# A decoder step with a width-31 depthwise convolution: one channel tile moves from GpSimd to products with diagonals on TensorE

## The chip, the cores and the metric

The kernel runs on one core of one Trainium2 chip. The metric is the device time of one execution in microseconds, the median of several runs. A core has five engines with queues of their own: TensorE (PE), VectorE (DVE), ScalarE (ACT), GpSimd (POOL) and SyncE (SP). [...] In this kernel SP does nothing but issue DMAs, in the order of its program.

## The reference

One inference step of two layers over 512 prompt tokens and 8 x 8 sample tokens, 576 columns in all, with 1024 channels, float32. Layer 0 mixes tokens with a recurrent state (RWKV), layer 1 with a causal Conformer convolution module; after each comes a gated feed-forward part with its own width-3 convolution. The change is in layer 1's mixer:

```
def _causal_dwconv(x, buf, w, b):            # w: (31, 1024), one filter of 31 taps for each channel
    xp = concatenate([buf, x], axis=1)       # 30 earlier rows in front (zeros for the prompt)
    y = depthwise_conv(xp, w)                # y[t, c] = sum over n of w[n, c] * xp[t + n, c]
    return y + b, xp[:, -30:]                # the last 30 rows are an output, the new state

def _conformer_conv(x, buf, w_in, b_in, dw_w, dw_b, ln_w, ln_b, w_out, b_out):
    h = x @ w_in + b_in                      # 1024 -> 2048
    h = h[..., :C] * sigmoid(h[..., C:])     # gated linear unit (glu)
    h, new_buf = _causal_dwconv(h, buf, dw_w, dw_b)
    h = silu(layernorm(h, ln_w, ln_b))       # mean and variance over the 1024 channels
    return h @ w_out + b_out, new_buf
```

## The kernel before, in words

Everything is held with channels on the 128 partitions, so 1024 channels are eight channel tiles (`KT`) of 128 x 576. The order of the work on each engine is written out by hand in one program per engine; a counting semaphore stands for each kind of event. The semaphore `tile_full` counts the PSUM tiles that PE has filled, `tile_read` those that another engine has read out; PSUM holds four tiles, and `begin(t)` in PE's program waits until tile t - 4 is read. `TB[name]` is the running number of the first tile of a step.

The mixer of layer 1 runs like this:

- `glu`: PE makes 16 products (L471 and L472, 512 and 64 columns), two for each channel tile. ACT evicts them to `gsig`, the second with a sigmoid (L1122, L1124). DVE multiplies the two and puts the result into `gb` (L1570, L1572), behind 30 columns of history; `glu_ready` counts the channel tiles.
- The depthwise convolution is divided by channel tile. DVE makes tiles 0, 2, 4, 6, 7 with 31 taps each, and the last 11 taps of tile 5: a tap is one multiply-add on 512 columns and one on 64 (L1615; the first tap of a tile L1617). DVE keeps two tiles in turn and does one glu step at every 16th tap. POOL makes tile 1: it multiplies into a scratch tile `ptmp` and adds that (L1706, L1707, L1711). PE makes the first 20 taps of tile 5 and all of tile 3, each tap a product of a 128 x 128 diagonal of the tap's weights with the shifted columns, summed up in PSUM (L797, L798). The diagonals come from ACT (L1117), a few ahead of each glu pair; ACT evicts the two PSUM tiles, adding the bias (L1127).
- `go`: DVE copies the newest rows of every channel tile together (`newest`, L1581 and L1583), PE transposes them (L483), ACT reads the two tiles into `ost` (L1131, L1133). SP then stores them: 73 DMAs, which are 8 for the prompt, 64 for the samples, and one copy of the older rows from input to output. Behind them SP loads the weights of `co` into a ring of four buffers.
- `ln`: PE sums the eight channel tiles with a matrix of 1/1024 (in the order 0, 2, 4, 6, 3, 1, 7, 5, each term waiting for its tile), ACT copies the mean (L1135), DVE subtracts it (L1630), ACT squares (L855), PE sums again, DVE takes the reciprocal (L1175) and scales (L1634), ACT applies silu (L1140).
- `co`: PE multiplies with the output weights, waiting for its first weight tile and for silu; then norms, the second feed-forward part, and the outputs.

What sets the order of SP's part:

```
            eng.wait_ge(sm["tile_read"], TB["go"] + 2)
            for kt in range(KT):
                store(out["p_glu"]...)
                for b in range(DB):
                    store(out["s_glu"]...)
            store(out["s_glu"][0, :, 0:NSTATE - DS, :], a["state_conv_glu"][0, :, DS:NSTATE, :])
            weights("co", a["conv_w_out"][0], range(KT))
```

Of the kernel before, what the change touches and what calls it, by code (L numbers as in the profile page):

```python
# [24 lines left out]
ALU = mybir.AluOpType  # L25
# [4 lines left out]
P = 128  # L30
D = 1024
SEQ = 512
DB, DS = 8, 8
DEC = DB * DS
T = SEQ + DEC
KT = D // P
# [4 lines left out]
CW = 31  # L41
# [83 lines left out]

DW_DVE, DW_POOL, DW_PE = (0, 2, 4, 6, 7), 1, (5, 3)
DW_TAPS = {5: 20, 3: CW}
DW_JOBS = [(kt, n) for kt in DW_PE for n in range(DW_TAPS[kt])]  # L130


# [6 lines left out]
TB = {}  # L139
# [31 lines left out]
A_FR = A_FO  # L171
# [5 lines left out]
A_SIG = A_CO + REG  # L177
GLU_EVERY = 16
A_DIAG = A_SIG + 2 * T
A_PTMP = A_DIAG + len(DW_JOBS) * P  # L180
assert A_PTMP + T <= A_FR
NSOUT = 2 * DB


def build(nc, a, out):
    with ExitStack() as ctx:
# [6 lines left out]
        def sem(name):  # L193
            return ctx.enter_context(nc.semaphore(name))
# [19 lines left out]
        def region(at, n=KT, w=T):  # L214
            return arena[:, at:at + n * w].rearrange("p (k t) -> p k t", t=w)
# [17 lines left out]
        gb = region(A_GB, KT, GB)  # L233
        gst = arena[:, A_GR:A_GR + NGS]
        cvo = region(A_CO)
        gsig = region(A_SIG, 2)
        gd = gb[:, :, NSTATE + SEQ:GB].rearrange("p k (b t) -> p k b t", b=DB)
# [29 lines left out]
        def pcol(name, i):  # L267
            return par[:, PCOL[name] + i:PCOL[name] + i + 1]

        def gain(n, kt):  # L270
# [3 lines left out]
                 "tile_full", "tile_read", "sq_ready", "sq_used", "x_ready", "h_ready", "xm_ready", "vec_done",  # L274
                 "v_ready", "wide_ready", "prep_sq", "prep_s", "prep_done", "kn_ready", "unit_done", "gath_ready",
                 "rk_ready", "sel_ready", "rstd_ready", "z_ready", "zeroed", "sd_turned", "sd_ready", "rf_ready",
                 "rows_ready", "snat_ready", "state_out", "glu_ready", "conv_done", "conv_pool", "pool_tap",
                 "diag_ready", "ln_v"]
        sm = {n: sem(n) for n in NAMES}
        w_in = [sem(f"w_in{i}") for i in range(RING)]  # L280
# [12 lines left out]
        def tset(t):  # L293
            return (t % 4) * 1024
# [163 lines left out]
        def _(pe):  # L458
# [5 lines left out]
            def product(t, terms, m=P, mark=None):  # L464

                begin(t)
                for i, (lhs, rhs, pre) in enumerate(terms):
                    for w, v in pre:
                        pe.wait_ge(w, v)
                    st, sp = i == 0, i == len(terms) - 1  # L470
                    pe.matmul(ps[0:m, tset(t):tset(t) + SEQ], lhs, rhs[:, 0:SEQ], start=st, stop=sp)  # L471
                    ins = pe.matmul(ps[0:m, tset(t) + SEQ:tset(t) + T], lhs, rhs[:, SEQ:T], start=st, stop=sp)  # L472
                    if mark is not None and not sp:
                        ins.then_inc(mark, 1)
                ins.then_inc(sm["tile_full"], 1)
# [177 lines left out]
            for k in range(KT):  # L653
                g, b = k % 2, 0
# [54 lines left out]
            for kt in range(KT):  # L709
                t = TB["pz"] + 3 * kt  # L710
# [79 lines left out]
            for m, kt in enumerate(DW_PE):  # L790
                t = TB["dw"] + m
                begin(t)
                pe.wait_ge(sm["glu_ready"], kt + 1)
                for n in range(DW_TAPS[kt]):
                    pe.wait_ge(sm["diag_ready"], job + 1)
                    st, sp = n == 0, n == DW_TAPS[kt] - 1
                    pe.matmul(ps[:, tset(t):tset(t) + SEQ], diag[:, job, :], gb[:, kt, n:n + SEQ], start=st, stop=sp)  # L797
# [10 lines left out]
            by = {kt: (sm["conv_done"], m + 1) for m, kt in enumerate(DW_DVE + DW_PE[:1])}  # L808

            by[DW_DVE[-1]] = by[DW_PE[0]]  # L810
            by[DW_PE[1]] = (sm["tile_read"], TB["dw"] + 2)
            by[DW_POOL] = (sm["conv_pool"], 1)
            product(TB["ln"], [(con[:, C_MEAN:C_MEAN + P], cvo[:, kt, :], [by[kt]]) for kt in (0, 2, 4, 6, 3, 1, 7, 5)])
            norm_sums("ln", first=1)
            gemm("co", cvo, (sm["z_ready"], KT))
# [344 lines left out]
        def _(dve):  # L1160
# [8 lines left out]
            def after():  # L1169
                if done[0]:  # L1170
                    dve.wait_ge(sm["vec_done"], done[0])
# [302 lines left out]
            for kt in range(KT):  # L1474
                t = TB["pz"] + 3 * kt
                g, b = tmp[:, 2 * (kt % 2), :], tmp[:, 2 * (kt % 2) + 1, :]
# [112 lines left out]

            turned, done_glu, step, waiting, active, last = False, 0, 0, [(kt, 0) for kt in DW_DVE] + [(DW_PE[0], DW_TAPS[DW_PE[0]])], [], {}  # L1590
            while waiting or active:
# [3 lines left out]
                while len(active) < 2 and waiting and waiting[0][0] < done_glu:  # L1595
                    kt, n = waiting.pop(0)
# [11 lines left out]
                kt, n = active.pop(0)  # L1608
                cd = cvo[:, kt, SEQ:T].rearrange("p (b t) -> p b t", b=DB)
                w = pcol("conv_dw_w", n * KT + kt)  # L1610
# [13 lines left out]
                    active.append([kt, n + 1])  # L1624
            dve.wait_ge(sm["tile_read"], TB["ln"] + 1)
            dve.wait_ge(sm["conv_done"], len(DW_DVE) + 1)
            dve.wait_ge(sm["conv_pool"], 1)
            after()
            for kt in range(KT):
                v.tensor_tensor(cvo[:, kt, :], cvo[:, kt, :], tmp[:, 3, :], ALU.subtract).then_inc(sm["ln_v"], 1)  # L1630
# [9 lines left out]
        @block.gpsimd  # L1640
        def _(pool):
            p = nc.gpsimd
            def ffn(l):
                w = FF[l]
                st = fst[:].rearrange("p (b w f) -> p b w f", b=DB, w=2)

                def decode(j):
                    return raw[:, j, 2 + SEQ:RAW].rearrange("p (b t) -> p b t", b=DB)

                def w_lo(at, i=None):  # L1650

                    pool.wait_ge(w["w_hi"], at + 1 + (0 if i is None else i * 4))
                    p.tensor_tensor(wsplit[:, at % 4, 1], ring[:, at % 2], wsplit[:, at % 4, 0].bitcast(F32), ALU.subtract)\  # L1653
                        .then_inc(w["w_lo"], 1)

                def tails(i, j):

                    pool.wait_ge(sm["tile_read"], i * 4 + (t0 + at + j + 1))
                    f = (j % 2) * FT + j // 2 + f0
                    o = fo[:, bass.ds(i * 2 + f, 1), :]  # L1660
                    p.tensor_copy(o[:, :, 0:2], raw[:, j:j + 1, SEQ:SEQ + 2]).then_inc(w["tails"], 1)
                    p.tensor_copy(o[:, :, 2:18].rearrange("p o (b t) -> p (o b) t", t=2), decode(j)[:, :, DS:DS + 2])\
                        .then_inc(w["tails"], 1)

                t0 = TB[f"f{l}"]
                for n in range(LOOK):
                    w_lo(n)
                pool.wait_ge(w["no_hist"], 4)
                pool.wait_ge(sm["tile_read"], TB[f"fst{l}"] + 2)
                for j in range(4):  # L1670
                    p.tensor_copy(decode(j)[:, :, 0:2], st[:, :, :, (j % 2) * FT + j // 2]).then_inc(w["hist_ready"], 1)
                at = 0
                for part, (f0, nf) in enumerate(PARTS):
                    last = part == len(PARTS) - 1
                    with pool.Fori(0, nf // 2 - last) as i:
                        for j in range(4):
                            w_lo(at + j + LOOK, i)
                            tails(i, j)

                            pool.wait_ge(w["conv_ready"], i * 4 + (2 * f0 + j + 1))  # L1680
                            pool.wait_ge(w["tails"], i * 8 + (4 * f0 + 2 * j + 2))
                            f = (j % 2) * FT + j // 2 + 2 + f0
                            src = st[:, :, :, bass.ds(i * 2 + f, 1)].rearrange("p b w o -> p b (w o)")
                            p.tensor_copy(decode(j)[:, :, 0:2], src).then_inc(w["hist_ready"], 1)  # L1684
                    if last:
                        for j in range(4):
                            w_lo(at + 2 * nf - 4 + j + LOOK)
                            tails(nf // 2 - 1, j)
                    at += 2 * nf
                    for n in range(KT):  # L1690
                        if at + n + LOOK < NFFN:
                            w_lo(at + n + LOOK)
                    at += KT

            ffn(0)

            kt = DW_POOL
            ptmp = arena[:, A_PTMP:A_PTMP + T]
            pool.wait_ge(sm["glu_ready"], kt + 1)
            for n in range(CW):  # L1700
                dst = ptmp if n else cvo[:, kt, :]
                w = pcol("conv_dw_w", n * KT + kt)
                add = pcol("conv_dw_b", kt) if n == 0 else 0.0
                if n > 1:
                    pool.wait_ge(sm["pool_tap"], 2 * n - 1)
                p.tensor_scalar(dst[:, 0:SEQ], gb[:, kt, n:n + SEQ], w, add, ALU.mult, ALU.add)  # L1706
                p.tensor_scalar(dst[:, SEQ:T].rearrange("p (b t) -> p b t", b=DB), gd[:, kt, :, n:n + DS], w, add, ALU.mult, ALU.add)\  # L1707
                    .then_inc(sm["pool_tap"], 1)
                if n:
                    pool.wait_ge(sm["pool_tap"], 2 * n)  # L1710
                    p.tensor_tensor(cvo[:, kt, :], cvo[:, kt, :], ptmp, ALU.add)\  # L1711
                        .then_inc(sm["pool_tap"] if n < CW - 1 else sm["conv_pool"], 1)
            ffn(1)


# [29 lines left out]
```

## Time and profile before

| what | us |
|---|---|
| median of three runs (2418.45 to 2422.42) | 2419.24 |
| span of the profiled execution, first to last instruction | 2418.1 |
| PE busy in it | 2176.1 (90%) |
| DVE busy | 1328.9 (55%) |
| ACT busy | 564.9 (23%) |
| POOL busy | 512.5 (21%) |

The profile is of one execution. Its times count from the span's start, and a busy engine is not always the one that the others wait for: the share on the chain of work that ended last says more. The mixer of layer 1 lies between 1555 and 1875 us. In the rows below an engine's "idle before" stands in square brackets, with the instruction that ended it; a queue with a q at the end (SPq) is the part of an engine that issues. One fp32 product has two rows in the trace (x2). [...]

### The profile page before, as it was taken

Reading aid. Unit: us, or ns where it says so; the run is one execution under the profiler, and the core shown is the slowest. Engines: PE = TensorE matmul, PEld = TensorE weight load, DVE = VectorE, ACT = ScalarE, POOL = GpSimd, SP = SyncE. Lnnn points to the kernel's source line nnn. Section 1 sums busy time; section 2 is a strip of 40 time slices with the busy share of each in tenths; the row PEclk is TensorE's granted clock in tenths of the full one; section 3 lists DMA queues with packets and bytes.
Section 4 is the critical chain, followed back from the end, with each engine's and each line's share of the span. In section 5 each row is a group of like instructions: output and inputs, shape, how many; then the busy total and the mean of one; then the engine's idle time right before and its main releaser. Section 6 shows DMA issues by size and latency. Waiting matters only on the chain.

```text
span 2418.1 us, 33008 instructions
## 1 busy us (share of the span) xinstructions
PE 2176.1 (90%) x12995; PEld 1753.6 (73%) x12995; DVE 1328.9 (55%) x2206; ACT 564.9 (23%) x903; POOL 512.5 (21%) x496
## 2 busy tenths in 40 slices
PE   5999999999998699979799998799959797999985
PEld 3555579999997345569799898555535597998985
DVE  5127345556665833078548365469970586284563
ACT  3203133232222020133222222321020432122122
POOL 0000000000000000024445343059200144354440
PEclk8999899999999876989899999899979898999998
DMA  4022100000000030112222221221011022222221
GB/s 128 21 60 60 35 1 10 10 1 10 1 10 1 0 85 9 50 44 70 86 72 78 88 70 53 66 61 42 1 54 53 26 79 78 75 82 79 79 61 46
DMA packets 228490, 116.90 MB, mean 48 GB/s; under 512 B 26065, under 2 KB 226217, under 8 KB 228233
## 3 DMA queue, kind: packets, MB, share of 16 engines
q1 hardware_dynamic: 228377, 115.31, 16.8%
q8 instruction: 81, 1.33, 0.2%
q14 instruction: 32, 0.26, 0.0%
HBM read 109.33 MB, written 6.67 MB: 48 GB/s over the span
## 4 chain that ended last, share of the span: by engine, by line
PE 62%; DVE 21%; issue 12%; ACT 3%; DVEq 1%; DMA 1%; POOL 0%; ACTq 0%; SPq 0%; POOLq 0%
PE ps L471 23%; PE ps L727 19%; PE ps L553 14%; DVE arena L1615 6%; PE ps L472 4%; DVE arena L1532 1%; DVE arena L1528 1%; DVE arena L1537 1%; DVE arena L1511 1%; DVE arena L1365 1%; ACT hidsplit L1083 1%; DVE tmp L1419 1%; DVE tmp L1175 1%; DVE arena L1512 1%; DVE tmp L1436 1%
## 5 line engine op out<-in xcount | busy, mean ns | idle before, releaser
L1653 POOL TENSOR_TENSOR wsplit<-arena,wsplit 128x1024 fp32r<-128x1024 f32 x136 | 325.4, 2393 | 1456.0 <-ACT wsplit L1053 1456.0
L727 PE MATMUL ps<-hsplit,wsplit 128*128 128x288 f32 x4224 | 575.9, 298 | 21.3 <-POOL wsplit L1653 19.8
L471 PE MATMUL ps<-arena 128*128 128x512 f32 (+4 forms) x1024 | 572.1, 642 | 18.2 <-ACT arena L1140 6.4
L727 PEld LDWEIGHTS ps<-hsplit,wsplit 128*128 128x128 f32 x4224 | 569.4, 190 | 24.3 <-POOL wsplit L1653 22.4
L553 PE MATMUL ps<-arena 128*128 128x128 f32 (+2 forms) x2992 | 392.8, 285 | 46.7 <-DVE arena L1365 14.9
L553 PEld LDWEIGHTS ps<-arena 128*128 128x128 f32 x2992 | 359.3, 194 | 76.9 <-DVE arena L1365 19.9
L472 PEld LDWEIGHTS ps<-arena 128*128 128x128 f32 (+4 forms) x1024 | 198.0, 193 | 261.4 <-issue 261.4
L727 PE MATMUL ps<-hidsplit,wsplit 128*128 128x288 f32 x2112 | 296.0, 304 | 48.9 <-DVE hidsplit L1541 48.9
L727 PEld LDWEIGHTS ps<-hidsplit,wsplit 128*128 128x128 f32 x2112 | 294.0, 196 | 50.3 <-DVE hidsplit L1541 50.3
L1053 ACT ACTIVATE wsplit<-arena 128x1024 fp32r<-128x1024 f32 x136 | 139.1, 1052 | 223.2 <-PE ps L727 212.5
L1615 DVE SCALAR_TENSOR_TENSOR arena<-arena,par 128x512 f32<-128x512 f32 x322 | 175.1, 623 | 0.1
L471 PEld LDWEIGHTS ps<-arena 128*128 128x128 f32 (+4 forms) x1024 | 158.3, 195 | 19.3 <-issue 18.7
L472 PE MATMUL ps<-arena 128*128 128x64 f32 (+4 forms) x1024 | 172.3, 251 | 0.0
L1175 DVE RECIPROCAL tmp<-tmp 128x576 f32<-128x576 f32 x9 | 33.8, 3753 | 228.6 <-ACT tmp L863 228.6
L1531 DVE SCALAR_TENSOR_TENSOR arena<-arena,par 128x512 f32<-128x512 f32 x176 | 140.1, 796 | 26.2 <-DVE arena L1528 6.7
L1527 DVE TENSOR_SCALAR arena<-arena,par 128x512 f32<-128x512 f32 x88 | 140.0, 1591 | 18.5 <-DVE arena L1513 18.5
L926 ACT ACTIVATE arena<-arena 64x256 f32<-64x256 f32 x148 | 61.4, 415 | 213.3 <-PE ps L553 211.0
L1551 DVE TENSOR_TENSOR arena<-arena,ps 128x576 f32<-128x576 f32 x32 | 24.1, 754 | 147.8 <-PE ps L727 147.8
L1083 ACT ACTIVATE hidsplit<-arena 128x576 f32 x44 | 30.2, 687 | 255.4 <-DVE arena L1537 255.4
L553 PE MATMUL ps<-tmp,arena 128*128 128x128 f32 (+2 forms) x432 | 86.6, 314 | 0.4 <-ACT arena L982 0.4
L1237 DVE SCALAR_TENSOR_TENSOR arena<-arena,par 128x576 f32<-128x576 f32 x48 | 35.4, 811 | 92.5 <-PE ps L472 92.4
L1684 POOL COPY arena<-arena 128x16 f32 x80 | 38.9, 486 | 200.6 <-DVE arena L1532 200.6
(203 smaller groups left out, 2012.5 us busy)
## 6 DMA issues: line engine op xcount, KB each, us to landing
arena<-ffn_w_in SPq DMA_DIRECT2D x88, 512.0 KB, 3.9
arena<-ffn_w_out SPq DMA_DIRECT2D x32, 512.0 KB, 4.0
arena<-conv_w_in SPq DMA_DIRECT2D x16, 512.0 KB, 4.0
arena<-ffn_w_out SPq DMA_DIRECT2D x16, 384.0 KB, 3.3
arena<-rwkv_wk SPq DMA_DIRECT2D x8, 512.0 KB, 5.7
arena<-rwkv_wr SPq DMA_DIRECT2D x8, 512.0 KB, 4.0
arena<-rwkv_wv SPq DMA_DIRECT2D x8, 512.0 KB, 3.9
arena<-rwkv_wo SPq DMA_DIRECT2D x8, 512.0 KB, 5.0
```

The source lines that it names most:

```text
L471: pe.matmul(ps[0:m, tset(t):tset(t) + SEQ], lhs, rhs[:, 0:SEQ], start=st, stop=sp)
L472: ins = pe.matmul(ps[0:m, tset(t) + SEQ:tset(t) + T], lhs, rhs[:, SEQ:T], start=st, stop=sp)
L553: return pe.matmul(o, lhs, rhs, start=start, stop=stop)
L727: ins = pe.matmul(ps[:, s + 512 * z:s + 512 * z + HALF], lhs(u, i), rhs[:, v, i, HALF * z:HALF * z + HALF], start=i == 0 and n == 0, stop= ...
L926: ins = f(dst[e:e + 64, k, e:e + 64], src[e:e + 64, k, tok], ACT.Copy)
L1053: f(wsplit[:, at % 4, 0], ring[:, at % 2], ACT.Copy).then_inc(FF[l]["w_hi"], 1)
L1083: f(hidsplit[:, 0, bass.ds(i * 2 + q, 1), :], cv[:, 2 * q:2 * q + 1, :], ACT.Copy).then_inc(w["hid_hi"], 1)
L1175: seq(v.reciprocal(tmp[:, 2, :], tmp[:, 2, :]))
L1527: v.tensor_scalar(cv[:, j, 0:SEQ], rp[:, 0:SEQ], tap(0), bias, ALU.mult, ALU.add).then_inc(chain, 1)
L1531: v.scalar_tensor_tensor(cv[:, j, 0:SEQ], rp[:, n:n + SEQ], tap(n), cv[:, j, 0:SEQ], ALU.mult, ALU.add).then_inc(chain, 1)
L1615: ins = v.scalar_tensor_tensor(dst, src, w, dst, ALU.mult, ALU.add)
L1653: p.tensor_tensor(wsplit[:, at % 4, 1], ring[:, at % 2], wsplit[:, at % 4, 0].bitcast(F32), ALU.subtract)\
```

## The change

Channel tile 1 is taken from POOL and given to PE as a third tile of the list `DW_PE`, with all 31 taps. POOL's loop, its scratch tile and its two semaphores go. What follows from the list follows without further edits: the number of diagonals rises from 51 to 82 (`DW_JOBS`), so ACT makes 11 instead of 7 ahead of each glu pair (five ahead of the last); PE has three depthwise tiles in PSUM (`TILES`, `("dw", len(DW_PE))`), ACT evicts three; the waits of the LayerNorm sum and of DVE for tile 1 are now on that eviction. DVE's program is the same but for this one wait.

```diff
--- before.py
+++ after.py
@@ -125,8 +125,8 @@
 
 
 
-DW_DVE, DW_POOL, DW_PE = (0, 2, 4, 6, 7), 1, (5, 3)
-DW_TAPS = {5: 20, 3: CW}
+DW_DVE, DW_PE = (0, 2, 4, 6, 7), (5, 3, 1)
+DW_TAPS = {5: 20, 3: CW, 1: CW}
 DW_JOBS = [(kt, n) for kt in DW_PE for n in range(DW_TAPS[kt])]
 
 
@@ -177,8 +177,7 @@
 A_SIG = A_CO + REG
 GLU_EVERY = 16
 A_DIAG = A_SIG + 2 * T
-A_PTMP = A_DIAG + len(DW_JOBS) * P
-assert A_PTMP + T <= A_FR
+assert A_DIAG + len(DW_JOBS) * P <= A_FR
 NSOUT = 2 * DB
 
 
@@ -274,7 +273,7 @@
                  "tile_full", "tile_read", "sq_ready", "sq_used", "x_ready", "h_ready", "xm_ready", "vec_done",
                  "v_ready", "wide_ready", "prep_sq", "prep_s", "prep_done", "kn_ready", "unit_done", "gath_ready",
                  "rk_ready", "sel_ready", "rstd_ready", "z_ready", "zeroed", "sd_turned", "sd_ready", "rf_ready",
-                 "rows_ready", "snat_ready", "state_out", "glu_ready", "conv_done", "conv_pool", "pool_tap",
+                 "rows_ready", "snat_ready", "state_out", "glu_ready", "conv_done",
                  "diag_ready", "ln_v"]
         sm = {n: sem(n) for n in NAMES}
         w_in = [sem(f"w_in{i}") for i in range(RING)]
@@ -809,7 +808,7 @@
 
             by[DW_DVE[-1]] = by[DW_PE[0]]
             by[DW_PE[1]] = (sm["tile_read"], TB["dw"] + 2)
-            by[DW_POOL] = (sm["conv_pool"], 1)
+            by[DW_PE[2]] = (sm["tile_read"], TB["dw"] + 3)
             product(TB["ln"], [(con[:, C_MEAN:C_MEAN + P], cvo[:, kt, :], [by[kt]]) for kt in (0, 2, 4, 6, 3, 1, 7, 5)])
             norm_sums("ln", first=1)
             gemm("co", cvo, (sm["z_ready"], KT))
@@ -1624,7 +1623,7 @@
                     active.append([kt, n + 1])
             dve.wait_ge(sm["tile_read"], TB["ln"] + 1)
             dve.wait_ge(sm["conv_done"], len(DW_DVE) + 1)
-            dve.wait_ge(sm["conv_pool"], 1)
+            dve.wait_ge(sm["tile_read"], TB["dw"] + 3)
             after()
             for kt in range(KT):
                 v.tensor_tensor(cvo[:, kt, :], cvo[:, kt, :], tmp[:, 3, :], ALU.subtract).then_inc(sm["ln_v"], 1)
@@ -1694,22 +1693,6 @@
 
             ffn(0)
 
-            kt = DW_POOL
-            ptmp = arena[:, A_PTMP:A_PTMP + T]
-            pool.wait_ge(sm["glu_ready"], kt + 1)
-            for n in range(CW):
-                dst = ptmp if n else cvo[:, kt, :]
-                w = pcol("conv_dw_w", n * KT + kt)
-                add = pcol("conv_dw_b", kt) if n == 0 else 0.0
-                if n > 1:
-                    pool.wait_ge(sm["pool_tap"], 2 * n - 1)
-                p.tensor_scalar(dst[:, 0:SEQ], gb[:, kt, n:n + SEQ], w, add, ALU.mult, ALU.add)
-                p.tensor_scalar(dst[:, SEQ:T].rearrange("p (b t) -> p b t", b=DB), gd[:, kt, :, n:n + DS], w, add, ALU.mult, ALU.add)\
-                    .then_inc(sm["pool_tap"], 1)
-                if n:
-                    pool.wait_ge(sm["pool_tap"], 2 * n)
-                    p.tensor_tensor(cvo[:, kt, :], cvo[:, kt, :], ptmp, ALU.add)\
-                        .then_inc(sm["pool_tap"] if n < CW - 1 else sm["conv_pool"], 1)
             ffn(1)
```

On PE, this is the place between the last tap of tile 3 and the LayerNorm sum. Lines L797 and L798 are the taps (L796 and L797 after the change, where the file is one line shorter above), L483 (L482) the transposes of `go`, L471 (L470) the first term of the sum. Before:

```order
L797 MATMUL ps<-arena 128x512 [waits diag_ready]
L798 MATMUL ps<-arena 128x64
L483 MATMUL ps<-con,arena 120x128 [waits tile_read,gath_ready]
L483 MATMUL ps<-con,arena 120x128
L483 MATMUL ps<-con,arena 128x128 [waits tile_read]
L483 MATMUL ps<-con,arena 128x128 x3
L471 MATMUL ps<-arena,con 128x512 [waits conv_done,tile_read]
```

And after it, from the last tap of tile 3 into the first taps of tile 1:

```order
L796 MATMUL ps<-arena 128x512 [waits diag_ready]
L797 MATMUL ps<-arena 128x64
L796 MATMUL ps<-arena 128x512 [waits diag_ready,glu_ready,tile_read]
L797 MATMUL ps<-arena 128x64
L796 MATMUL ps<-arena 128x512 [waits diag_ready]
L797 MATMUL ps<-arena 128x64
```

Where the transposes stood, 31 pairs for tile 1 begin; the transposes and the sum follow behind them.

On ACT, the rows from the last but one glu pair to the copy of the mean (L1117 diagonals, L1122 and L1124 glu evictions, L1127 depthwise evictions, L1131 and L1133 the reads of `go`, L1135 the mean). Before:

```order
L1117 ACTIVATE arena<-con,par 128x128 x7
L1122 ACTIVATE arena<-ps,par 128x576 [waits tile_full,glu_ready]
L1124 ACTIVATE arena<-ps,par 128x576 [waits tile_full]
L1117 ACTIVATE arena<-con,par 128x128 x2
L1122 ACTIVATE arena<-ps,par 128x576 [waits tile_full,glu_ready]
L1124 ACTIVATE arena<-ps,par 128x576 [waits tile_full]
L1127 ACTIVATE arena<-ps,par 128x576 [waits tile_full] x2
L1131 ACTIVATE ost<-ps 120x256 [waits out_done,tile_full]
L1133 ACTIVATE ost<-ps 128x512 [waits tile_full]
L1135 ACTIVATE tmp<-ps 128x576 [waits tile_full]
```

And after it, the same stretch, one line number lower:

```order
L1116 ACTIVATE arena<-con,par 128x128 x11
L1121 ACTIVATE arena<-ps,par 128x576 [waits tile_full,glu_ready]
L1123 ACTIVATE arena<-ps,par 128x576 [waits tile_full]
L1116 ACTIVATE arena<-con,par 128x128 x5
L1121 ACTIVATE arena<-ps,par 128x576 [waits tile_full,glu_ready]
L1123 ACTIVATE arena<-ps,par 128x576 [waits tile_full]
L1126 ACTIVATE arena<-ps,par 128x576 [waits tile_full] x3
L1130 ACTIVATE ost<-ps 120x256 [waits out_done,tile_full]
L1132 ACTIVATE ost<-ps 128x512 [waits tile_full]
L1134 ACTIVATE tmp<-ps 128x576 [waits tile_full]
```

More diagonals stand ahead of each pair, and a third eviction stands between PE's depthwise tiles and the reads of `go`. SP's program is word for word the same.

## Rows read from the trace of the kernel before

**Rows 1.** The page: the span, and the chain that ended last by engine

```profile
span 2418.1 us, 33008 instructions
...
PE 62%; DVE 21%; issue 12%; ACT 3%; DVEq 1%; DMA 1%; POOL 0%; ACTq 0%; SPq 0%; POOLq 0%
```

**Rows 2.** Windows of PE: stretch, length, busy, granted clock, DMA share, GB/s

```profile
1564.37:1751.70 187.33, 187.31 (x694) 1.00 0.13 36
1751.70:1760.40 8.70, 0.00 (x0) 0.67 0.00 0
1769.90:1781.04 11.14, 0.01 (x1) 0.73 0.07 16
1781.04:1785.55 4.51, 4.49 (x8) 0.52 0.06 14
1785.55:1798.40 12.85, 10.52 (x32) 0.87 0.62 181
```

**Rows 3.** Waits of PE, 1550 to 1810: total, times, longest

```profile
PE ps L471 <- DVE arena L1615: 11.1, 1, 11.1
PE ps L483 <- DVE arena L1583: 8.8, 1, 8.8
```

**Rows 4.** Timeline of PE: start, us, line, shapes, count [idle before]

```profile
1696.34 1.08 PE L797 MATMUL ps<-arena 128*128 128x512 f32 x2
...
1751.35 0.33 PE L798 MATMUL ps<-arena 128*128 128x64 f32 x2
1760.44 1.53 PE L483 MATMUL ps<-con,arena 128*120 128x128 f32 x6 [8.77 <-DVE arena L1583]
...
1804.80 2.05 PE L471 MATMUL ps<-arena 128*128 128x512 f32 x2 [6.41 <-ACT arena L1140]
```

**Rows 5.** Windows of the tap line L1615 alone, before and while POOL works

```profile
1577.16:1593.40 16.24, 12.96 (x30) 1.00 0.21 60
1628.99:1652.30 23.31, 23.31 (x32) 1.00 0.22 64
```

**Rows 6.** Timeline of DVE: two glu steps and the last taps

```profile
1576.16 0.69 DVE L1570 TENSOR_TENSOR arena<-arena 128x512 f32<-128x512 f32 x1 [13.09 <-ACT arena L1124]
...
1593.47 0.69 DVE L1570 TENSOR_TENSOR arena<-arena 128x512 f32<-128x512 f32 x1 [2.67 <-ACT arena L1124]
...
1760.30 20.69 DVE L1615 SCALAR_TENSOR_TENSOR arena<-arena,par 128x512 f32<-128x512 f32 x48
```

**Rows 7.** Windows of POOL: its tile

```profile
1594.00:1710.00 116.00, 109.78 (x92) 1.00 0.15 45
```

**Rows 8.** Timeline of ACT: diagonals, a glu eviction, a depthwise eviction, the reads of go

```profile
1576.03 2.15 ACT L1117 ACTIVATE arena<-con,par 128x128 f32<-128x128 f32 x7
1584.10 0.74 ACT L1122 ACTIVATE arena<-ps,par 128x576 f32<-128x576 f32 x1 [5.92 <-PE ps L472]
...
1751.71 0.74 ACT L1127 ACTIVATE arena<-ps,par 128x576 f32<-128x576 f32 x1 [32.79 <-PE ps L798]
1761.16 0.39 ACT L1131 ACTIVATE ost<-ps 120x256 f32<-120x256 f32 x1 [8.71 <-PE ps L483]
1762.01 0.60 ACT L1133 ACTIVATE ost<-ps 128x512 f32<-128x512 f32 x1 [0.47 <-PE ps L483]
```

**Rows 9.** Timeline of SP: the first stores, a slower eight, the weights of co

```profile
1762.64 0.33 SPq L348 DMA_DIRECT2D out_p_glu<-ost  x1
1763.01 2.66 SPq L348 DMA_DIRECT2D out_s_glu<-ost  x8
...
1766.08 2.94 SPq L348 DMA_DIRECT2D out_s_glu<-ost  x8
...
1788.74 53.45 SPq L303 DMA_DIRECT2D arena<-conv_w_out  x8
```

**Rows 10.** Landing of conv_w_out tiles: the first one alone, then all eight

```profile
DMA to landing us min/median/max: 7.5/7.5/7.5
...
DMA to landing us min/median/max: 3.7/5.6/9.9
```

## The prediction

> **What bounds the stage now.** I read the page first, then TensorE's (PE's) busy time by stretch, its waits and its timeline, then VectorE (DVE), GpSimd (POOL), ScalarE (ACT) and SyncE (SP) in the same 250 us, because the diff touches only the depthwise stage and what comes right behind it. The page says that PE carries 62% and DVE 21% of the chain that ended last [rows 1]. So PE leads nearly everywhere, and this stage is a place where DVE takes over.
>
> The stretches show where. PE is busy without a gap at granted clock 1.00 from 1564.37 to 1751.70: the glu product, and from 1696.34 the two depthwise tiles. Then it does nothing for 8.70 us, works 9.5 us, and does nothing for 11.14 us [rows 2]. The two idle stretches are the waits for DVE of 8.8 and 11.1 us [rows 3]: the first for the gathered newest rows (L1583), the second for DVE's last tap (L1615). DVE's last block of taps starts at 1760.30 and lasts 20.69 us, to 1781.0 [rows 6]; PE resumes at 1781.04 with the last two terms of the LayerNorm sum. The reader is to see that DVE ends last here, with some 20 us of PE time free in front of it, and that POOL is not the one waited for: its tile is done by 1710 [rows 7].
>
> A second chain runs beside it, on SP. Its first store of the glu state goes out at 1762.64, 0.03 us after ACT's second read of the `go` tiles ended (1762.01 + 0.60). Seventy-three stores (8 + 64 + 1) follow one another, and only behind them, at 1788.74, the first weight tile of the next product `co` [rows 8, 9]. That tile takes 7.5 us to land [rows 10], so it is there at 1796.2. PE starts `co` at 1804.80 [rows 4] because the normalized input comes then. The weights have 8.6 us of slack.
>
> **The change part by part.**
>
> *PE gains a third product.* The two existing ones are 51 taps from 1696.34 to 1751.35 + 0.33 = 1751.68 [rows 4], 55.34 us or 1.085 us a tap, across POOL's end. Thirty-one more are 33.64 us. They stand in front of the `go` transposes, so PE ends its taps at 1751.68 + 33.64 = 1785.32 where it ended at 1751.68. Nothing in front of them gets earlier: PE was already without a gap from 1564.37 on, so a faster DVE gives the glu product nothing. The free 8.70 + 11.14 = 19.8 us cover part; the rest sticks out.
>
> *ACT gains 31 diagonals and one eviction.* Seven diagonals take 2.15 us and ACT then idles 5.92 us until its next tile [rows 8]; eleven take 3.4 us. Cost nothing, hidden by that idle time; without the cover it would be 1.2 us for each of seven glu pairs. The eviction (0.74 us, as the one at 1751.71 [rows 8]) lies between the product's end and the reads of `go`.
>
> *POOL loses its tile, DVE gets faster.* POOL worked 109.8 us of the 116 us in which it made the tile [rows 7]. A DVE tap, one instruction on 512 and one on 64 columns, costs 12.96 / 15 = 0.864 us before POOL starts, 23.31 / 16 = 1.46 us while it works, and 20.69 / 24 = 0.862 us afterwards [rows 5, 6]. So DVE gets back some half a microsecond on each tap that ran beside POOL. It cannot use all of it, since a glu step stands behind every 16 taps and these come from PE 17.31 us apart (1576.16, 1593.47 [rows 6]), and 16 × 0.864 us and a glu step of under a microsecond, less than 15 us, is less. The eighth glu step then falls at 1576.16 + 7 × 17.31 = 1697.3, with 96 of the 5 × 31 + 11 = 166 taps done; the other 70 take 60.4 us, and the glu step and the copies of the newest rows about a microsecond each: DVE ends near 1759.8, 21 us earlier. The newest rows, with 24 taps behind them, are ready near 1738. Both now wait for PE, so this gain is worth nothing on the path.
>
> [...]
>
> *Chain one, through the LayerNorm.* From 1785.32 PE does six transposes (0.8 us, half of the 1.53 us that they took right after an idle stretch [rows 4]) and all eight terms of the sum, now without waiting: the third tile's eviction is done 0.8 us after the product, behind transposes and five other terms. A term has the shapes of a tap, so eight are 8 × 1.085 = 8.7 us, and the sum is there at 1794.8 instead of 1785.5: 9.3 us later. [...] So 1.8 us come back, and the input of `co` is ready 7.5 us later, at 1812.3.
>
> *Chain two, through SP.* SP issues in order and its wait is on the `go` tiles, which now lie behind the third product. Product ends 1785.32, ACT evicts it (0.74), reads the first `go` tile (0.39) and the second (0.60): 1787.1. The first store goes out there instead of at 1762.64, 24.4 us later. The stores are the same, 26.10 us of issue, so the first weight tile is issued at 1813.2 and lands 7.5 us on, at 1820.7. That is behind the 1812.3 of chain one: the weights' slack of 8.6 us is used up and they become what PE waits for. `co` starts at 1820.7 instead of 1804.80, **15.9 us later**. The next tiles are issued right behind it and none landed later than 9.9 us after its issue [rows 10]; PE takes 8 × 1.085 us for each product, so they do not add. PE begins `co` after an idle stretch in either case. Behind `co` nothing that the diff touches is left and every step follows its predecessor as before, so the delay stays to the end.
>
> Bounds: eight stores took 2.66 to 2.94 us, so the stores are 0.3 us less to 2.3 us more; a `conv_w_out` tile landed in 3.7 to 9.9 us [rows 10], so −3.8 to +2.4 us. I take the first tile's own landing, 7.5 us, because the same copy of older rows stands in front of it. Ends: 11.8 to 20.6 us.
>
> **Sum.** The profiled span is 2418.1 us; the runs' median, 2419.24, is 1.1 us above it. 2418.1 + 15.9 = 2434.0 of span, 2435.1 as a median. Own range 2430 to 2440.
>
> **Rivals.**
>
> B: only chain one counts, because the weights come in time (SP's stores go out faster, or the first tile lands early enough). Then +7.5, 2426.7 us. For it: the LayerNorm chain is what decides now. Against it: it wants 8.4 us less in the stores and the landing, and the even rows of the stores leave 0.3 and the fastest landing 3.8.
>
> C, the other side: the third product disappears in PE's idle stretches and DVE's 21 us count. Place: PE between 1751.7 and 1781.0. With taps that cost nothing the sum ends right behind DVE, and `co` starts with the weights at 1751.7 + 1.8 + 26.1 + 7.5 = 1787.1, so 2401 us; at half the price they come at 1803.9, 2418 us. It decides at 0.57 us a tap, where the weights come at 1804.8 as `co` does now. Against it: 102 rows of this very line at 1.085 us a tap with PE at full clock.
>
> D: the granted clock falls under a longer unbroken stretch. It stood at 1.00 for 187 us, and the stretch becomes some 230. At the low clock in the added taps, +34 us more, 2469 us. No row of this stage speaks for it.
>
> **Chances.** Forecast 0.86, B 0.07, C 0.03, D 0.04. A measurement of this kernel can tell about 0.2%, 4.8 us, from no change. A, B and D are slower by more, 0.95 with a little of B below the line; C is 0.03 faster and the remaining 0.02 same. The range reaches from B to the upper bound of the forecast: 2426 to 2440.
>
> **What would show it.** In the profile of the changed kernel: taps in a row of 82 at 1.085 us ending near 1785; no wait of PE for L1615 or the newest rows; DVE taps at 0.86 us throughout, ending near 1760, with waits of 2 to 3 us at each glu step; the first glu store near 1787, the first `conv_w_out` issue near 1813; PE idle for about 15 us before `co`, with ACT's normalized input done some 8 us before that idle ends. I am wrong if `co` starts when ACT's input comes (B), if PE does not reach the transposes near 1785 (C or D), or if a later stage takes the 16 us back.

## The result and the profile after

| kernel | median us | runs | ratio to the kernel before, 95% interval |
|---|---|---|---|
| before | 2420.83 | 4 | |
| changed | 2436.32 (2435.27 to 2438.1) | 4 | 1.0069, 1.0055 to 1.0083 |

The changed kernel is slower by 15.5 us by the medians. The prediction was 2435.1 us, 15.9 us over the median of three runs that it started from. The profiled executions differ a little more, 2435.0 against 2418.1 us of span: 16.9 us.

The page of the changed kernel, its chain that ended last by engine (the row of before is in [rows 1]):

```profile
PE 67%; DVE 15%; issue 12%; ACT 3%; DVEq 1%; SPq 1%; DMA 1%; POOL 0%; ACTq 0%; POOLq 0%
```

PE's share rises from 62% to 67%, DVE's falls from 21% to 15%: the stage in which DVE took over has gone to PE. SPq, at 0% before, now has 1%: the issue queue of SP has come onto the chain.

PE's waits in the mixer, 1550 to 1830 (total, times, longest), to be read beside [rows 3]:

```profile
PE ps L470 <- DMA arena<-conv_w_out: 15.5, 1, 15.5
PE ps L470 <- DVE arena L1183: 5.6, 1, 5.6
PE ps L470 <- ACT tmp L854: 2.3, 1, 2.3
```

Both waits for DVE in this stage, 8.8 and 11.1 us, are gone; the 5.6 us are those ahead of the glu product, which were there before. In their place is a wait that did not exist: 15.5 us for the DMA of the `co` weights.

PE's stretches, as in [rows 2] (length, busy, granted clock as a share of full speed, DMA share, GB/s):

```profile
1564.37:1785.50 221.13, 221.13 (x823) 1.00 0.11 31
1785.50:1794.60 9.10, 9.09 (x37) 1.00 0.05 13
1796.90:1805.80 8.90, 8.84 (x32) 1.00 0.07 18
1805.80:1821.29 15.49, 0.00 (x1) 0.62 0.40 118
```

The reader is to see one unbroken stretch of 221 us at clock 1.00, up to the end of the third product, then the LayerNorm sums at 1.00 too, and then 15.5 us with nothing.

PE's timeline at both ends of that (columns as in [rows 4]):

```profile
1785.00 0.33 PE L797 MATMUL ps<-arena 128*128 128x64 f32 x2
1785.17 0.82 PE L482 MATMUL ps<-con,arena 128*120 128x128 f32 x6
...
1821.29 2.05 PE L470 MATMUL ps<-arena 128*128 128x512 f32 x2 [15.52 <-DMA arena<-conv_w_out]
...
1823.44 2.02 PE L470 MATMUL ps<-arena 128*128 128x512 f32 x2
...
1825.58 1.53 PE L470 MATMUL ps<-arena 128*128 128x512 f32 x2
...
1827.11 1.08 PE L470 MATMUL ps<-arena 128*128 128x512 f32 x2
```

The last tap ends at 1785.33, the six transposes take 0.82 us, and `co` starts at 1821.29 where it started at 1804.80: 16.5 us later.

DVE's first instruction of the stage (the scaling of the norm ahead of the glu products), in the kernel before and then in the changed one:

```profile
1554.74 5.92 DVE L1184 SCALAR_TENSOR_TENSOR arena<-x,par,tmp 128x576 f32<-128x576 f32 x8
```

```profile
1554.82 5.92 DVE L1183 SCALAR_TENSOR_TENSOR arena<-x,par,tmp 128x576 f32<-128x576 f32 x8
```

From there to the first `co` product it is 250.1 us before and 266.5 us after, 16.4 us more. This length, called the stage's length below, is given for the experiments too, because their profiled executions differ by up to 3.1 us in what lies ahead of the stage.

DVE's timeline, two glu steps, taps behind them, and the last taps (columns as in [rows 6]):

```profile
1593.59 0.69 DVE L1569 TENSOR_TENSOR arena<-arena 128x512 f32<-128x512 f32 x1 [2.67 <-ACT arena L1123]
...
1594.45 12.96 DVE L1614 SCALAR_TENSOR_TENSOR arena<-arena,par 128x512 f32<-128x512 f32 x30
...
1628.20 0.69 DVE L1569 TENSOR_TENSOR arena<-arena 128x512 f32<-128x512 f32 x1 [15.54 <-ACT arena L1123]
...
1738.63 20.68 DVE L1614 SCALAR_TENSOR_TENSOR arena<-arena,par 128x512 f32<-128x512 f32 x48
```

Thirty instructions, 15 taps, take 12.96 us where POOL used to work beside them (19.62 us before for the same 30), and DVE ends at 1738.63 + 20.68 = 1759.3 instead of 1781.0. It now waits 2.6 to 3.5 us at a usual glu step and 15.54 us at the fourth, in front of which it has only one tap to do.

ACT's timeline: diagonals, the third depthwise eviction, the two reads of `go`, the first silu (columns as in [rows 8]):

```profile
1576.15 3.31 ACT L1116 ACTIVATE arena<-con,par 128x128 f32<-128x128 f32 x11
1584.22 0.74 ACT L1121 ACTIVATE arena<-ps,par 128x576 f32<-128x576 f32 x1 [4.76 <-PE ps L471]
...
1785.37 0.74 ACT L1126 ACTIVATE arena<-ps,par 128x576 f32<-128x576 f32 x1 [32.80 <-PE ps L797]
1786.01 0.38 ACT L1130 ACTIVATE ost<-ps 120x256 f32<-120x256 f32 x1
1786.27 0.60 ACT L1132 ACTIVATE ost<-ps 128x512 f32<-128x512 f32 x1
...
1811.16 6.18 ACT L1139 ACTIVATE arena<-arena,par 128x576 f32<-128x576 f32 x8 [3.10 <-DVE arena L1633]
```

Eleven diagonals take 3.31 us and still leave 4.76 us of idle time (5.92 us before). The first silu starts at 1811.16; before, `co` followed it by 1.02 us.

SP's timeline, the first stores, the slowest eight, the weights (columns as in [rows 9]), and under it the landing of the first two weight tiles (us from issue, minimum, median, maximum):

```profile
1786.90 0.33 SPq L347 DMA_DIRECT2D out_p_glu<-ost  x1
1787.27 2.66 SPq L347 DMA_DIRECT2D out_s_glu<-ost  x8
...
1806.37 3.23 SPq L347 DMA_DIRECT2D out_s_glu<-ost  x8
...
1813.58 45.46 SPq L302 DMA_DIRECT2D arena<-conv_w_out  x8
```

```profile
DMA to landing us min/median/max: 7.6/8.2/8.9
```

The stores begin at 1786.90 instead of 1762.64 and take 26.7 us of issue; 1813.58 and 7.6 us are 1821.2, when PE starts.

### The profile page after: what moved, and what is told of

The parts are those of the page before. It is cut to its first block, busy times and chain, and to the rows that moved or that the text cites. A ratio compares the mean times of both kernels' runs of the same rounds, so it can differ in the third digit from the quotient of the medians.

```text
span 2435.0 us, 33195 instructions
## 1 busy us (share of the span) xinstructions
PE 2203.4 (90%) x13119; PEld 1769.5 (73%) x13119; DVE 1288.1 (53%) x2206; ACT 573.7 (24%) x935; POOL 402.5 (17%) x404
## 3 DMA queue, kind: packets, MB, share of 16 engines
q8 instruction: 82, 1.34, 0.2%
## 4 chain that ended last, share of the span: by engine, by line
PE 67%; DVE 15%; issue 12%; ACT 3%; DVEq 1%; SPq 1%; DMA 1%; POOL 0%; ACTq 0%; POOLq 0%
PE ps L470 25%; PE ps L726 19%; PE ps L552 14%; PE ps L471 4%; PE ps L796 3%; DVE arena L1531 1%; DVE arena L1527 1%; DVE arena L1536 1%; DVE arena L1510 1%; DVE arena L1364 1%; SPq L347 1%; ACT hidsplit L1082 1%; DVE tmp L1418 1%; DVE arena L1511 1%; DVE tmp L1435 1%
## 5 line engine op out<-in xcount | busy, mean ns | idle before, releaser
L470 PE MATMUL ps<-arena 128*128 128x512 f32 (+4 forms) x1024 | 572.9, 643 | 27.3 <-DMA arena<-conv_w_out 15.5
L726 PE MATMUL ps<-hsplit,wsplit 128*128 128x288 f32 x4224 | 576.0, 298 | 21.3 <-POOL wsplit L1652 19.8
L471 PEld LDWEIGHTS ps<-arena 128*128 128x128 f32 (+4 forms) x1024 | 198.1, 193 | 261.8 <-issue 261.8
L470 PEld LDWEIGHTS ps<-arena 128*128 128x128 f32 (+4 forms) x1024 | 158.7, 196 | 28.5 <-issue 27.8
L471 PE MATMUL ps<-arena 128*128 128x64 f32 (+4 forms) x1024 | 172.5, 251 | 0.0
L1530 DVE SCALAR_TENSOR_TENSOR arena<-arena,par 128x512 f32<-128x512 f32 x176 | 140.1, 796 | 26.2 <-DVE arena L1527 6.7
L1614 DVE SCALAR_TENSOR_TENSOR arena<-arena,par 128x512 f32<-128x512 f32 x322 | 139.1, 507 | 0.1
L796 PE MATMUL ps<-arena 128*128 128x512 f32 x164 | 88.1, 619 | 0.0
```

The costliest lines, as they stand in the source:

```text
L726: ins = pe.matmul(ps[:, s + 512 * z:s + 512 * z + HALF], lhs(u, i), rhs[:, v, i, HALF * z:HALF * z + HALF], start=i == 0 and n == 0, stop= ...
L1530: v.scalar_tensor_tensor(cv[:, j, 0:SEQ], rp[:, n:n + SEQ], tap(n), cv[:, j, 0:SEQ], ALU.mult, ALU.add).then_inc(chain, 1)
L1614: ins = v.scalar_tensor_tensor(dst, src, w, dst, ALU.mult, ALU.add)
```

## The experiments

Each experiment was measured in turn with the kernel before on the same chip, whose median there was 2420 to 2421 us; ratios are to it. The theory is that of the prediction: PE's third product puts off the `go` tiles, SP's order puts the weights of `co` behind them and 73 stores, and DVE's regained time is off the path.

**The weights ahead of the stores.** On SP, in the changed kernel:

```diff
+            weights("co", a["conv_w_out"][0], range(KT), upto=RING)
             eng.wait_ge(sm["tile_read"], TB["go"] + 2)
             ...
-            weights("co", a["conv_w_out"][0], range(KT))
+            weights("co", a["conv_w_out"][0], range(KT), first=RING)
```

> Changed kernel, but SP issues the first four weight tiles of co ahead of its wait for the go tiles, so ahead of the 73 stores. Theory (the weights behind the stores set the start of co): co starts when ACT's normalized input is there, which in the changed kernel was 9.1 us before PE got its weights (ACT's silu from 1811.2, co from 1821.3), so 2436.3 - 9 = 2427 us. Rival (the third product alone is the delay, and the weights only happen to come at that time): within 1 us of the changed kernel, 2436 us.

Measured: 2427.78 us, 1.0029 (1.0018 to 1.004). Its waits of PE from 1690 to 1835, and SP's first weights and first store:

```profile
PE ps L471 <- ACT arena L1140: 6.4, 1, 6.4
PE ps L471 <- ACT tmp L855: 2.3, 1, 2.3
```

```profile
1689.75 4.82 SPq L302 DMA_DIRECT2D arena<-conv_w_out  x4
1784.09 0.36 SPq L347 DMA_DIRECT2D out_p_glu<-ost  x1
```

The 15.5 us wait for the DMA is gone and PE waits for ACT's silu again, 6.4 us as before the change. By the medians, 8.5 of the 15.5 us by which the kernel had become slower were SP's order; the remaining 7 are the LayerNorm chain behind the third product, the 7.5 us of the prediction's chain one. The stage's length, 257.4 us (1552.01 to 1809.36), says the same: 9.1 us less than in the changed kernel, 7.3 us more than before.

**The same edit in the kernel before.**

> Kernel before with the same reordering on SP alone. Theory: its weights had 8.6 us of slack, so nothing moves, 2420 to 2422 us. Rival (the order on SP is worth the same in any version, for instance because the stores disturb the weight loads): about 9 us faster, 2412 us.

Measured: 2420.09 us, 1.0001 (0.9992 to 1.001). The stage's length is 250.1 us, as without the edit. The order on SP costs nothing there; its weights had slack, and the change used it up.

**POOL kept busy.** The changed kernel, with POOL doing its old loop on tile 1 into a buffer that nobody reads:

```diff
+            pool.wait_ge(sm["glu_ready"], kt + 1)
+            for n in range(CW):
+                dst = ptmp if n else idle            # idle, ptmp: hg[:, 0, :], hg[:, 1, :]
+                p.tensor_scalar(dst[:, 0:SEQ], gb[:, kt, n:n + SEQ], w, add, ALU.mult, ALU.add)
+                ...
```

> Changed kernel, but POOL does its old loop of tile 1 into a buffer that nobody reads. Theory (PE and then SP set the end, so DVE's 21 us are off the path): DVE's taps take 1.3 to 1.5 us again beside POOL and end near 1781, and the time stays within 1.5 us of the changed kernel, 2436 us. Rival (DVE's gain already pays for part of the third product): up to 21 us slower, 2446 to 2457 us.

Measured: 2434.69 us, 1.0068 (1.0054 to 1.0082), which is not to be told from the changed kernel. DVE's last taps and its next instruction, and PE's wait:

```profile
1758.02 20.67 DVE L1614 SCALAR_TENSOR_TENSOR arena<-arena,par 128x512 f32<-128x512 f32 x48
1793.07 5.44 DVE L1629 TENSOR_TENSOR arena<-arena,tmp 128x576 f32<-128x576 f32 x8 [14.37 <-ACT tmp L1134]
```

```profile
PE ps L470 <- DMA arena<-conv_w_out: 15.3, 1, 15.3
```

DVE's taps ended at 1778.7 there, in an execution in which the stage lay 2.2 us earlier, so some 21.6 us later than in the changed kernel, and no engine waited for it: PE reached the sum's last terms only behind its third product, and its wait is still the one for the weights. The stage's length is 266.2 us for 266.5. What DVE gained from an idle POOL was worth nothing in the changed kernel.

**One tap instead of 31.** `DW_TAPS[1] = 1`: the third product and its PSUM tile stay, with one tap and its diagonal; the other 30 diagonals go with their taps.

> Changed kernel with one tap instead of 31 in tile 1's product; the other 30 taps are left out of the output. Theory (33.6 us of PE, 1.085 us a tap, are the whole price; the order on SP then decides): PE ends its taps near 1753, DVE near 1760, the first store goes out near 1754.6, the weights land near 1788.3 and co starts there, 16.4 us before the kernel before: 2404 us. Rival (something else of the change costs the time, the diagonals or the third PSUM tile): not below 2415 us. Second rival (the stores do not matter): co starts near 1780, 2396 us.

Measured: 2401.96 us, 0.9926 (0.9911 to 0.9941). PE's transposes of `go` and the start of `co`, and SP's weights:

```profile
1749.62 0.83 PE L482 MATMUL ps<-con,arena 128*120 128x128 f32 x6
...
1785.68 2.04 PE L470 MATMUL ps<-arena 128*128 128x512 f32 x2 [13.78 <-DMA arena<-conv_w_out]
```

```profile
1778.06 7.45 SPq L302 DMA_DIRECT2D arena<-conv_w_out  x4
```

Thirty taps less are 34.4 us less by the medians, against 30 × 1.085 = 32.6 us of products. The stage's length, 1551.73 to 1785.68, is 234.0 us, 32.5 us less than in the changed kernel, so the products account for all of it there. The price lies in the taps, not in the list of three or its PSUM tile. This run does not separate a tap from its diagonal; that the diagonals cost nothing is read from the changed kernel's trace, where PE runs through all 82 taps without a wait, busy for 88.99 of the 88.99 us from 1696.34 to 1785.33. And `co` still starts with the weights, 7.6 us after their issue, though ACT's silu began at 1777.29: this kernel too waits for SP's order. What it would gain without that, an estimate of 7.4 us from the 1.02 us between silu and `co` elsewhere, was not measured.

**Tile 1 divided between PE and DVE.** PE makes 15 taps of tile 1, DVE the other 16 behind PE's eviction, POOL stays idle; the LayerNorm sum takes the tiles that DVE ends last at its end. Once with the weights ahead of the stores, once without.

```diff
-DW_DVE, DW_PE = (0, 2, 4, 6, 7), (5, 3, 1)
-DW_TAPS = {5: 20, 3: CW, 1: CW}
+DW_DVE, DW_PE = (0, 2, 4, 6, 7), (5, 1, 3)
+DW_TAPS = {5: 20, 1: 15, 3: CW}
...
-[(kt, 0) for kt in DW_DVE] + [(DW_PE[0], DW_TAPS[DW_PE[0]])]
+[(kt, 0) for kt in DW_DVE] + [(kt, DW_TAPS[kt]) for kt in DW_PE[:2]]
```

> POOL idle as in the changed kernel, but tile 1 is divided: PE makes its first 15 taps (order on PE: tile 5 with 20 taps, tile 1 with 15, tile 3 with 31) and DVE the other 16, and the first four weight tiles of co are issued ahead of the stores. Theory (DVE's regained 21 us are worth something once PE does not carry the whole tile, and the weights are out of the way): PE ends its taps at 1751.7 + 15 x 1.085 = 1768, DVE near 1774.4, the LayerNorm sum ends near 1777.5 instead of 1785.5 and the second sum saves 1.8 us more, so co starts 9 to 10 us before the kernel before: 2411 us. Rival (DVE's regained time is lost in its waits for glu steps and for PE's partial tile): not faster than before, 2418 to 2422 us.

> The same division of tile 1, with SP's order as it was. Theory (the weights follow the go tiles by 1.8 + 26.1 + 7.5 us): the go tiles come at 1768 instead of 1751.7 plus DVE's wait, the weights near 1803.5, so co starts about 1 us before the kernel before: 2419 us. Rival (the stores do not matter here): 2411 us, as with the weights first.

Measured: 2411.93 us, 0.9965 (0.9952 to 0.9979) with the weights first; 2420.22 us, 1.0001 (0.9992 to 1.001) without. The start of `co` in the first and in the second:

```profile
1794.54 2.05 PE L471 MATMUL ps<-arena 128*128 128x512 f32 x2 [6.41 <-ACT arena L1139]
```

```profile
1802.95 2.05 PE L470 MATMUL ps<-arena 128*128 128x512 f32 x2 [15.04 <-DMA arena<-conv_w_out]
```

With the weights out of the way the division pays, 8.6 us by the medians against the kernel before: DVE, faster without POOL (12.96 us for 15 taps, 0.864 us each), can take 16 of tile 1's taps off PE. With the old order on SP the same division gains nothing: PE waits 15.0 us for the DMA. Both came within 1.3 us of what was expected.

**DVE without waits for glu pairs.** The balanced version with the weights first, in an order in which DVE always has a tile at hand:

```diff
-DW_DVE, DW_PE = (0, 2, 4, 6, 7), (5, 1, 3)
-DW_TAPS = {5: 20, 1: 15, 3: CW}
-GLU_EVERY = 16
+DW_DVE, DW_PE = (0, 1, 2, 4, 6), (5, 7, 3)
+DW_TAPS = {5: 2, 7: 18, 3: CW}
+GLU_EVERY = 19
```

> As the balanced version with the weights first, but DVE's order is changed so that it always has a tile to work on while it waits for glu pairs: DVE makes tiles 0, 1, 2, 4, 6 with a glu step at every 19th tap (19 x 0.864 + 0.92 = 17.3 us, PE's pace), PE makes 2 taps of tile 5, 18 of tile 7 and all of tile 3, DVE the rest of 5 and 7. Theory (the time that DVE regains from an idle POOL went mostly into its waits for glu pairs, 32 us in the changed kernel, and is worth something once these are gone): DVE ends near 1756 and PE's taps near 1752, the LayerNorm sum near 1761 instead of 1777 in the balanced version, so 2396 us. Rival (DVE's taps get slower or the glu product is held up when DVE never idles): 2405 us or more.

Measured: 2393.65 us, 0.9901 (0.9885 to 0.9918), the fastest of all. DVE's waits from 1570 to 1765 in the changed kernel and then here (total, times, longest):

```profile
DVE arena L1569 <- ACT arena L1123: 45.4, 8, 15.5
```

```profile
DVE arena L1569 <- ACT arena L1123: 13.5, 3, 13.1
...
DVE arena L1614 <- ACT arena L1126: 1.3, 1, 1.3
```

Of the changed kernel's 45.4 us, 13.1 are the wait for the first pair, and the other 32.3 lie between taps. Here 0.4 us of these are left, and 1.3 us for PE's part of tile 5. The taps kept their pace (19 of them, less the first, in 15.53 / 18 = 0.863 us each), so nothing was lost to DVE working without a pause. PE has 51 taps here, as many as before the change, and the stage's length is 223.8 us, 26.3 us less than before; what is gone are PE's two waits for DVE, 19.9 us, and products at the low clock behind them (granted 0.52 in 1781.04 to 1785.55 [rows 2]). What this order would bring in the kernel before, with POOL at work, was not measured.

## Why the prediction was right

The mechanism and its size both came as forecast; the terms of the sum were within 0.6 us. What it missed, one sign and one term, did not enter the sum or was small.

- *PE's third product*: worked out to end at 1785.32, measured 1785.33. That the taps, and not the list of three, carry the price is shown by the kernel with one tap. The granted clock stayed at 1.00 through 221 us, so rival D fell; so did C, since the 82 taps took 1.084 us each (1.085 before).
- *ACT's diagonals hidden*: eleven took 3.31 us for 3.4 worked out, and 4.76 of the 5.92 us of idle time were left. Right.
- *DVE's gain worth nothing on the path*: DVE ended at 1759.3 for 1759.8 worked out. The kernel with POOL kept busy shows the conclusion: DVE some 21.6 us later, time the same. The waits of DVE explain why 21.7 us were gained and not more: before, it waited 13.7 us behind its first glu step (2.67 us in [rows 6], and 11.0 us at the fourth step), afterwards 32.3 us. 21.7 and 18.6 us are 40 us of faster work, of which almost half went into waiting for glu pairs.
- *A sign that was off*: DVE was to wait 2 to 3 us at each glu step, and at the fourth it waited 15.54 us, since only the first tap of tile 2 lies between the third and the fourth. The count of 96 taps by the eighth step had this in it, so DVE's end came out right all the same.
- *Chain one*: the input of `co` was to be ready at 1812.3; the first silu at 1811.16 and the 1.02 us that lay behind it before make 1812.2. That alone would have been rival B's 2426.7 us; the run with the weights first measured 2427.8. The 1.8 us in it that were to come back are the difference between the 10.52 us for which the second sum kept PE busy before, at granted clock 0.87 [rows 2], and eight terms of 1.085 us; no run has this sum alone with and without an idle stretch in front. In the changed kernel it kept PE busy for 8.84 us at granted clock 1.00, so 1.7 us came back.
- *Chain two*: the first store came 24.3 us later for 24.4 worked out, the stores took 26.7 us for 26.1 (one group of eight took 3.23 us instead of 2.66), the landing 7.6 us for 7.5. `co` started 16.5 us later instead of 15.9.
- *A term set at nothing*: `co` starts at the low clock in both kernels (granted 0.50 in 1804.80 to 1809.10 before, 0.55 in 1821.29 to 1827.10 after), but its third term, 1.17 us before, took 1.53 us. The start, 16.5 us later including the 0.1 us by which the whole stage began later in this execution, and these 0.4 us make up the 16.9 us of span; in the medians, 15.5 us, they are not to be told apart. Why the third term took longer stays open: the idle stretch in front was longer, but the third term took 1.08 us behind 13.8 us of idle time (one tap) and 1.89 us behind 15.0 us (the division with the old order on SP).
- *DVE beside POOL*: 1.46 us a tap while POOL works and 0.864 us without it were read before the change. With POOL idle a tap took 0.864 us all through the stage (12.96 us for 15, 13.82 us for 16), and in the kernel with POOL kept busy 1.34 to 1.39 us again, as the mean of blocks of 14 to 16 taps that ran wholly beside POOL. What makes it so is shown by no run. The 21.7 us by which DVE ended earlier did not count for the time, since PE's end hid them.

No later stage gave anything back: the delay of the first `co` product and that of the whole differ by less than half a microsecond.

## What to carry to other kernels

Work moved off a slow engine has to be priced on the engine that receives it, against the time for which that engine stands idle in the stage: here 33.6 us of products met 19.8 us of idle time, and the 40 us that DVE regained ended in its own waits. Then follow everything that hangs on the receiving engine's end, the DMA queue included: a queue that issues in order turned a late transpose into late weights (issued from 1813.58 on instead of from 1788.74), and one moved line of loads was worth more than the rest of the delay. Here the idle POOL paid only when the split and the order were made anew; split by measured prices (1.085 us a tap on PE, 0.863 on DVE), with DVE's waits filled and the weights issued early, the kernel with an idle POOL was 26 us faster than the kernel before instead of 15 us slower.

## What the runs showed of the hardware

- A tap of two instructions takes 0.863 us on DVE alone and, as the mean of blocks of 14 to 16 taps, 1.31 to 1.46 us beside POOL, while POOL needed 3.5 us for the same tap on average (109.8 us for 31), and 2.57 us in the stretch from 1617.13 to 1627.40, in which DVE stood idle: each slows the other. Over the stage POOL's tile cost DVE 40 us, in which DVE alone would do 46 taps; POOL made 31. If DVE has work to fill that time, POOL here costs more taps than it makes; the fastest kernel above has it idle.
- Small stores cost SP mostly 0.33 us of issue each, at 4 KB and at 15 KB alike, and 73 of them hold up what stands behind for 26.1 to 26.7 us, with the DMA engines hardly used (share 0.06 from 1762.64 to 1788.74 before the change).
